# Gate and up slabs of a two-block transformer kernel computed as seven products of halves instead of eight

## The chip, the cores and the metric

The kernel runs on one core of a Trainium2 chip, in one launch. The metric is device time in microseconds, the median of three runs. The profile is one execution taken by the hardware profiler.

## The reference

Two blocks run one after the other on 256 tokens of width 1024, in float32. The first block has two layers, and carries two streams of 256 tokens: the latents (`lat`) and a context (`cx`). Each layer puts both streams through a gated feed-forward, a token mixer with a two-way scan over chunks, and a second feed-forward. The second block has attention, a convolution, a memory attention and a mixture of 32 experts. The change touches the feed-forwards of the first block alone:

```python
D_MODEL = 1024; SEQ = 256; DEPTH = 2; D_FF = 2816
def _swiglu(h, w1, w3, w2):
    return (jax.nn.silu(h @ w1) * (h @ w3)) @ w2

lat = lat + 0.5 * ml[2] * _swiglu(_modulate(lat, norm_ffn1_g[l], ml[0], ml[1]), *ffn1)
cx  = cx  + 0.5 * mc[2] * _swiglu(_modulate(cx,  norm_ffn1_g[l], mc[0], mc[1]), *ffn1)
...
lat = lat + 0.5 * ml[8] * _swiglu(_modulate(lat, norm_ffn2_g[l], ml[6], ml[7]), *ffn2)
```

## The kernel before

The work is cut into **slabs**, one for each 1 MB piece of weights. A gate slab is 256 output columns of `w1` (128 partitions x 8 blocks of the contraction x 256 columns), an up slab the same of `w3`. A feed-forward has 11 pairs of one gate and one up slab, and then 12 down slabs. A **run** is named by (layer, stream, which of the two feed-forwards): stream 0 is the latents, held in `h`, stream 1 the context, held in a part of `ring` that the loads don't use.

The order is one list of stages, made by `first_order` (L196 to L268) and walked by each engine with its own code: TensorE, ScalarE, VectorE, GpSimd and the load queue each take from it what is theirs, strictly in that order, and wait for each other by semaphores. `spread_out` puts a **side chain** between the slabs of a run, one bundle of stages after a slab: in the runs (0,0,0), (0,1,1) and (1,1,0) it is a scan of the other stream's mixer. For each of four heads it holds two `decay` stages (VectorE makes exponents; at the odd one ScalarE takes their exponential, L1552 to L1554), `times` (VectorE L1771, GpSimd L2427), two `score` stages (TensorE L1191 to L1208, VectorE reduces), `value` and `head`. The run (0,0,0) has in its stream (0,1) a `gmlp` stage (TensorE L1172, VectorE L1777) ahead of the first decay.

A gate or up slab on TensorE (L1122) is 16 matrix products of 128x128 weights with 256 columns of tokens, into one of four PSUM banks. The profile shows every float32 product as two MATMUL rows, so that a slab is 32 rows. Behind a gate slab ScalarE writes `sil`, the silu of the bank (L1486). Behind an up slab VectorE multiplies `sil` with the bank into `hid` (L1771, 128x512). Nothing else of VectorE belongs to a slab, and TensorE waits for either of them only when it comes to the same bank again, four slabs later.

The loads go through a ring of `RING` = 5 places of 1 MB; the load of slab k waits until TensorE has finished slab k-5 (L798). `ada` slabs, which make the modulation vectors, use the same ring but take TensorE about 0.5 us each.

## Time and profile before

| | us |
|---|---|
| median of 3 runs | 3049.12 |
| lowest, highest | 3047.38, 3049.76 |
| span of the profiled execution | 3046.6 |
| TensorE busy | 2881.2 |
| VectorE busy | 916.5 |
| ScalarE busy | 539.0 |
| mean granted clock of TensorE | 0.974 |

The span is the time from the first instruction to the last. The median lies 2.5 us above it, which is what lies around the span. The mixture of experts takes the last 440 us or so; it waits for loads of weights at about 430 GB/s.

### The profile page before, as it was taken

To read this page: it belongs to the slowest core of one execution; us is meant where nothing else is said; L and a number is where in the kernel's file an instruction comes from. 1 tells how busy PE (TensorE), PEld (TensorE's weight loads), DVE (VectorE), ACT (ScalarE), POOL (GpSimd) and SP (SyncE) were. 2 spreads that over 40 slices of the span, in tenths; PEclk is the share of its full clock that TensorE was granted. 3 is DMA by queue.
4 is the path that set the end of the run, shared out by engine and by line. 5 is a ranking of instruction groups with operands and counts; after the bars stand their busy time and mean duration, and the time that the engine had idled before them with its cause. 6 is when DMAs were issued, how large, how long until landed. Compare 5 with 4: busy or idle time off the path is not lost.

```text
span 3046.6 us, 36306 instructions
## 1 busy us (share of the span) xinstructions
PE 2881.2 (95%) x15970; PEld 2403.4 (79%) x15970; DVE 916.5 (30%) x1686; ACT 539.0 (18%) x784; POOL 120.7 (4%) x192
## 2 busy tenths in 40 slices
PE   8999999999999999999999999999999999866766
PEld 6888888888888888888888888878888888533333
DVE  3864034331433215300014433510036412210111
ACT  2101222123211101010033206210012240200000
POOL 0000012100211000000001210000000000000000
PEclk9999999999999999999999999999999999987788
DMA  9775443344333566554444344354433238899998
GB/s 401 282 270 181 152 140 133 128 152 152 138 135 128 207 249 228 178 218 150 154 152 150 133 144 152 138 223 152 151 138 125 97 104 338 350 431 431 429 430 371
DMA packets 74128, 641.25 MB, mean 210 GB/s; under 512 B 8304, under 2 KB 9584, under 8 KB 21232
## 3 DMA queue, kind: packets, MB, share of 16 engines
q1 hardware_dynamic: 71376, 631.55, 54.8%
q10 hardware_dynamic: 2592, 7.33, 0.6%
q8 instruction: 129, 2.11, 0.3%
q14 instruction: 31, 0.25, 0.0%
HBM read 637.80 MB, written 1.05 MB: 210 GB/s over the span
## 4 chain that ended last, share of the span: by engine, by line
PE 86%; DMA 12%; DVE 1%; issue 0%; ACT 0%; SPq 0%; DVEq 0%; ACTq 0%
PE ps L1122 42%; PE ps L1144 18%; DMA work<-in_w_moe 11%; PE ps L1319 7%; PE ps L1132 3%; PE ps L1155 3%; PE ps L1349 2%; PE ps L953 2%; PE ps L1208 1%; PE ps L975 1%; DMA ring<-in_w_ada 1%; PE ps L1326 1%; PE ps L1080 0%; PE ps L1294 0%; PE ps L1297 0%; PE ps L1385 0%
## 5 line engine op out<-in xcount | busy, mean ns | idle before, releaser
L1122 PE MATMUL ps<-h,ring 128*128 128x256 f32 x3456 | 755.8, 380 | 7.0 <-ACT h L1526 2.9
L1122 PEld LDWEIGHTS ps<-h,ring 128*128 128x128 f32 x3456 | 654.5, 190 | 102.2 <-issue 8.7
L1122 PE MATMUL ps<-ring 128*128 128x256 f32 x2560 | 559.0, 379 | 0.0
L1144 PE MATMUL ps<-work,ring 128*128 128x256 f32 x2464 | 537.8, 379 | 0.0
L1122 PEld LDWEIGHTS ps<-ring 128*128 128x128 f32 x2560 | 484.0, 190 | 67.7 <-issue 1.9
L1144 PEld LDWEIGHTS ps<-work,ring 128*128 128x128 f32 x2464 | 466.3, 190 | 64.5 <-issue 2.1
L1771 DVE TENSOR_TENSOR work<-work,ps 128x512 f32<-128x512 f32 (+1 forms) x153 | 88.0, 575 | 713.9 <-PE ps L1122 637.6
L1319 PE MATMUL ps<-h,ring 128*128 128x256 f32 x928 | 205.0, 379 | 0.5 <-DVE h L1777 0.5
L1319 PEld LDWEIGHTS ps<-h,ring 128*128 128x128 f32 x928 | 174.8, 190 | 27.5 <-issue 4.2
L1777 DVE SCALAR_TENSOR_TENSOR work<-work,ring 128x1024 f32<-128x1024 f32 x140 | 173.5, 1281 | 1.7
L1486 ACT ACTIVATE work<-ps 128x512 f32<-128x512 f32 x77 | 46.0, 597 | 707.4 <-PE ps L1122 707.3
L1771 DVE TENSOR_TENSOR work<-work 128x128 f32<-128x128 f32 (+5 forms) x449 | 154.8, 401 | 47.5 <-ACT eb L1554 24.9
L2427 POOL TENSOR_TENSOR work<-work 128x128 f32<-128x128 f32 x168 | 100.0, 632 | 1690.3 <-ACT work L1552 1690.3
L953 PE MATMUL ps<-ring,work 128*32 128x256 f32 x1024 | 73.9, 452 | 34.2 <-DMA ring<-in_w_moe 33.9
L953 PE MATMUL ps<-work 128*32 128x256 f32 x992 | 71.6, 444 | 36.5 <-DMA work<-in_w_moe 35.8
L953 PEld LDWEIGHTS ps<-ring,work 128*32 128x32 f32 x1024 | 40.7, 129 | 66.6 <-issue 54.0
L953 PEld LDWEIGHTS ps<-work 128*32 128x32 f32 x992 | 40.1, 127 | 66.2 <-issue 53.2
L1777 DVE SCALAR_TENSOR_TENSOR x<-ps,mod,x 128x256 f32<-128x256 f32 x48 | 21.0, 480 | 234.2 <-PE ps L1144 166.0
L975 PE MATMUL ps<-work 128*32 128x512 f32 x288 | 49.7, 855 | 29.9 <-DMA work<-in_w_moe 29.5
L1730 ACT ACTIVATE work<-ps 32x256 f32<-32x256 f32 x64 | 24.0, 374 | 299.3 <-PE ps L953 298.9
L2368 DVE COPY work<-ps 128x128 f32<-128x128 f32 x32 | 9.3, 292 | 214.1 <-PE ps L962 214.1
L1349 PE MATMUL ps<-work,ring 128*128 128x256 f32 x320 | 70.2, 380 | 1.6 <-DVE work L1771 1.6
(287 smaller groups left out, 2176.8 us busy)
## 6 DMA issues: line engine op xcount, KB each, us to landing
ring<-in_w SPq DMA_DIRECT2D x182, 1024.0 KB, 4.8
work<-in_w_moe SPq DMA_DIRECT2D x22, 4096.0 KB, 33.6
ring<-in_w_moe SPq DMA_DIRECT2D x22, 4096.0 KB, 33.2
ring<-in_w_in SPq DMA_DIRECT2D x80, 1024.0 KB, 4.8
ring<-in_w SPq DMA_DIRECT2D x56, 896.0 KB, 4.7
work<-in_w_ada SPq DMA_DIRECT2D x40, 1024.0 KB, 6.8
ring<-in_w_ada SPq DMA_DIRECT2D x32, 1024.0 KB, 4.9
ring<-in_w_out SPq DMA_DIRECT2D x16, 1024.0 KB, 4.9
```

The lines of the kernel that those rows point to most:

```text
L953: last = nc.tensor.matmul(ps[i * CAP:i * CAP + CAP, g % 2, 0:256], hg[:, q % 2, k, e * CAP:e * CAP + CAP], w[i][:, k * 256:k * 256 + 256], ...
L975: last = nc.tensor.matmul(ps[e * CAP:e * CAP + CAP, 2 + half, :], hv[:, q % 2, e, k, :], w[e][:, k * 512:k * 512 + 512], start=(k == 0), s ...
L1122: last = nc.tensor.matmul(ps[:, b, c * L:c * L + L], w[:, k * L + c * P:k * L + c * P + P], hs[cols][:, k, :], start=(k == 0), stop=(k == ...
L1132: last = nc.tensor.matmul(ps[:, b, t * L:t * L + L], hs[stage[2]][:, k, t * P:t * P + P], w[:, k * L:k * L + L], start=(k == 0), stop=(k = ...
L1144: last = nc.tensor.matmul(ps[:, b, c * L:c * L + L], w[:, k * L + c * P:k * L + c * P + P], hid[:, k0 + k, :], start=(k0 + k == 0 and c == 0),
L1155: last = nc.tensor.matmul(ps[:, b, c * L:c * L + L], w[:, k * L + c * P:k * L + c * P + P], hs[s][:, k, :], start=(k == 0), stop=(k == KD ...
L1319: last = nc.tensor.matmul(ps[:, b, c * L:c * L + L], w[:, k * L + c * P:k * L + c * P + P], hs[0][:, k, :], start=(k == 0), stop=(k == KD ...
L1349: last = nc.tensor.matmul(ps[:, b, c * L:c * L + L], w[:, k * L + c * P:k * L + c * P + P], src[:, k, :], start=(k == 0), stop=(k == kn - 1))
L1486: nc.scalar.activation(sil[:, nth % 2, :], ps[:, b, :], ACT.Silu).then_inc(ev_a, 1)
L1771: return nc.vector.tensor_tensor(o, i0, i1, op)
L1777: return nc.vector.scalar_tensor_tensor(o, i0, s, i1, op0, op1)
L2427: nc.gpsimd.tensor_tensor(keys, keys, k_in, ALU.mult)
```

## The change

64 of the 154 gate and up slabs are computed in another way, a form of Strassen's product with seven products of halves in place of eight (`HALVED`): pairs 1 to 10 of the run (1,0,0), pairs 2 to 10 of (1,0,1), pairs 3, 5, 7, 9 of (0,0,0) and of (1,1,0), pairs 2, 4, 6, 8, 10 of (0,1,1). The slab's weights are four quarters, b11 to b22 (4 blocks of the contraction by 128 columns), the tokens four quarters, a11 to a22 (4 blocks by 128 tokens). `ON_POOL` is empty, so that all sums are VectorE's.

- `halves`, once for each run: VectorE makes s1 to s4, sums and differences of the quarters of the tokens, four operations of 128x512.
- `combine`, once for each slab: VectorE makes t3, b12-b11, t2 and t4 of the quarters of the weights, four operations of 128x512. It stands ahead of the slab before its own.
- TensorE: 28 products of 128x128 weights with 128 columns, into two banks, bx and by. The first two groups need only the weights and tokens, the third waits for `halves`, the next three for `combine`, and the last for `one_out`.
- ScalarE: a copy of one quarter of bx (128x128), which is `one_out`; behind a gate slab then a silu of the sums in SBUF.
- VectorE: three sums of 128, 128 and 256 elements and one of 384 for each slab; behind an up slab the product into `hid`.
- The ring has 4 places for loads in place of 5; the fifth holds the sums of the weights.

```diff
-RING = 5
+RING = 4
+HALVED = {(0, 0, 0): range(3, 11, 2), (0, 1, 1): range(2, 11, 2), (1, 1, 0): range(3, 11, 2), (1, 0, 0): range(1, 11), (1, 0, 1): range(2, 11)}
...
+def with_halves(plan):
...
+        ready = max(n for n in range(slabs[mine[0]]) if plan[n] == ("norm", l, s, 2 * j))
+        busy = [n for n in range(slabs[mine[0]]) if plan[n][0] == "gmlp"]
+        at = max([slabs[mine[0] - 2], ready + 1] + ([busy[-1] + 1] if l == 0 else []))
+        before[at].append(("halves", *run))
+        for i in mine:
+            before[max(slabs[i - 1], at)].append(("combine", *plan[slabs[i]]))
...
+                        product(bx, 3, b11, a11)
+                        product(bx, 0, b21, a12)
+                        pe.wait_ge(halves_done, at.halves_at[stage[1:4]] + 1)
+                        product(bx, 2, b22, s4).then_inc(x_mm, 1)
+                        engine, made = at.combined[stage]
+                        pe.wait_ge(combined_p if engine == "p" else combined_d, made)
+                        product(by, 2, b12, s1)
+                        product(by, 1, t3, s3)
+                        product(by, 0, t2, s2).then_inc(y_mm, 1)
+                        pe.wait_ge(one_out, nth + 1)
+                        product(bx, 1, t4, a22).then_inc(fb_slab, 1)
...
+                    elif is_halved(stage):
+                        nth, which = at.gate_at[stage[1:]][1], int(kind == "up")
+                        act.wait_ge(x_mm, at.halved[n] + 1)
+                        if not which:
+                            act.wait_ge(ev_d, at.up_at[nth - 1])
+                        nc.scalar.activation(part_sums[:, which, 1, :], ps[:, at.group[n] % 4, 3 * P:4 * P], ACT.Copy
+                                             ).then_inc(one_out, 1)
+                        if not which:
+                            act.wait_ge(ev_d, at.sums_at[n])
+                            nc.scalar.activation(sil[:, 0, :], sil[:, 0, :], ACT.Silu).then_inc(ev_a, 1)
...
+                    elif kind == "combine" and not on_pool(stage[1:]):
...
+                        tt(t3, b12, b22, sub).then_inc(dve_own, 1)
+                        third = S.next(dve_own)
+                        tt(b12, b12, b11, sub)
+                        dve.wait_ge(dve_own, third)
+                        own(tt(t2, b11, t3, sub))
+                        tt(t4, b21, t2, sub).then_inc(combined_d, 1)
+                    elif is_halved(stage):
...
+                        dve.wait_ge(one_out, at.halved[n] + 1)
+                        dve.wait_ge(y_mm, at.halved[n] + 1)
+                        own(tt(both[:, 0, :], both[:, 1, :], ps[:, by, 0:P], add))
+                        own(tt(both[:, 2, :], both[:, 0, :], ps[:, by, P:2 * P], add))
+                        tt(both[:, 3:5, :], pair, ps[:, by, 2 * P:3 * P].unsqueeze(1).to_broadcast([P, 2, P]), add).then_inc(ev_d, 1)
+                        dve.wait_ge(fb_slab, at.slab[n] + 1)
+                        dve.wait_ge(ev_d, at.sums_at[n] - 1)
+                        tt(total[:, 0:3 * P], total[:, 0:3 * P], ps[:, bx, 0:3 * P], add).then_inc(ev_d, 1)
```

**TensorE, run (0,0,0), from the `gmlp` stage on.** Before, slab 3 of this run (gate of pair 3) follows as 16 products of 256 columns:

```order
L1172 MATMUL ps<-wsbs,work 128x128 [waits gm_v,const_in]
L1172 MATMUL ps<-wsbs,work 128x128 x7
L1122 MATMUL ps<-h,ring 128x256 [waits w_full2,ev_a]
L1122 MATMUL ps<-h,ring 128x256 x15
L1122 MATMUL ps<-h,ring 128x256 [waits w_full3,ev_a]
L1122 MATMUL ps<-h,ring 128x256 x15
```

The same place in the changed kernel:

```order
L1286 MATMUL ps<-wsbs,work 128x128 [waits gm_v,const_in]
L1286 MATMUL ps<-wsbs,work 128x128 x7
L1214 MATMUL ps<-h,ring 128x128 [waits w_full2,ev_a]
L1214 MATMUL ps<-h,ring 128x128 x7
L1214 MATMUL ps<-work,ring 128x128 [waits halves_done]
L1214 MATMUL ps<-work,ring 128x128 x3
L1214 MATMUL ps<-work,ring 128x128 [waits combined_d]
L1214 MATMUL ps<-work,ring 128x128 x11
L1214 MATMUL ps<-h,work 128x128 [waits one_out]
L1214 MATMUL ps<-h,work 128x128 x3
```

The slab now stops at three places inside itself for VectorE and ScalarE.

**VectorE, the same run, from the `gmlp` stage to the first decay.** Before, the decay (L1786 is its first line) follows at once:

```order
L1771 TENSOR_TENSOR work<-work,ps 128x512
L1777 SCALAR_TENSOR_TENSOR pmt<-ps,vec,wsbs 128x256 x4
L1771 TENSOR_TENSOR ring<-pmt,work 128x1024
L1786 SCALAR_TENSOR_TENSOR work<-ring,work 128x256
L1771 TENSOR_TENSOR be<-work 128x2
```

In the changed kernel:

```order
L1895 TENSOR_TENSOR ring<-pmt,work 128x1024
L1895 TENSOR_TENSOR work<-h 128x512 x2
L1895 TENSOR_TENSOR work<-work,h 128x512
L1895 TENSOR_TENSOR work<-h,work 128x512
L1895 TENSOR_TENSOR ring<-ring 128x4x128 x3
L1895 TENSOR_TENSOR work<-ring 128x512
L1910 SCALAR_TENSOR_TENSOR work<-ring,work 128x256
```

`halves` (three rows) and the `combine` of gate 3 (two rows) have moved in ahead of it.

**VectorE, the same run, between the first decay and the second.** Before:

```order
L2009 COPY work<-work 128x2x64
L1771 TENSOR_TENSOR work<-work 128x2x64 x2
L1771 TENSOR_TENSOR work<-be,work 128x2x64
L1786 SCALAR_TENSOR_TENSOR work<-ring,work 128x256
L1771 TENSOR_TENSOR be<-work 128x2
```

In the changed kernel:

```order
L1895 TENSOR_TENSOR work<-be,work 128x2x64
L1895 TENSOR_TENSOR ring<-ring 128x4x128 x3
L1895 TENSOR_TENSOR work<-ring 128x512
L1895 TENSOR_TENSOR work<-work,ps 128x128 x2
L1895 TENSOR_TENSOR work<-work,ps 128x256
L1895 TENSOR_TENSOR work<-work,ps 128x384
L1910 SCALAR_TENSOR_TENSOR work<-ring,work 128x256
```

The `combine` of up 3 (two rows) and the four sums of gate 3 (three rows), which wait for TensorE, now stand between the two decays.

**ScalarE, the same run, around the second decay.** Before, the exponentials stand between the silus of gates 3 and 4 (L1486), and TensorE needs neither at once:

```order
L1486 ACTIVATE work<-ps 128x512 [waits ev_d,fb_slab] x2
L1552 ACT_TABLE_LOAD
L1552 ACTIVATE work<-work 128x2304 [waits dec_in]
L1553 ACTIVATE work<-work 128x2304
L1554 ACTIVATE eb<-be 128x4
L1486 ACT_TABLE_LOAD [waits ev_d]
L1486 ACTIVATE work<-ps 128x512 [waits fb_slab]
```

In the changed kernel:

```order
L1600 ACTIVATE work<-ps 128x128 [waits ev_d,x_mm]
L1604 ACTIVATE work<-work 128x512 [waits ev_d]
L1676 ACT_TABLE_LOAD
L1676 ACTIVATE work<-work 128x2304 [waits dec_in]
L1677 ACTIVATE work<-work 128x2304
L1678 ACTIVATE eb<-be 128x4
L1600 ACTIVATE work<-ps 128x128 [waits x_mm]
L1610 ACT_TABLE_LOAD [waits ev_d]
```

The copy of up 3 (the second L1600), for which TensorE waits inside the slab, stands behind the three exponentials.

## Rows read from the trace of the kernel before

**Rows 1.** The page: busy us (share), chain by engine, VectorE's wait for TensorE.
```profile
span 3046.6 us, 36306 instructions
PE 2881.2 (95%) x15970; PEld 2403.4 (79%) x15970; DVE 916.5 (30%) x1686; ACT 539.0 (18%) x784; POOL 120.7 (4%) x192
PE 86%; DMA 12%; DVE 1%; issue 0%; ACT 0%; SPq 0%; DVEq 0%; ACTq 0%
L1771 DVE TENSOR_TENSOR work<-work,ps 128x512 f32<-128x512 f32 (+1 forms) x153 | 88.0, 575 | 713.9 <-PE ps L1122 637.6
```

**Rows 2.** Timeline, TensorE: start, length, line, out<-in, shape, count; four stretches.
```profile
416.56 1.95 PE L1172 MATMUL ps<-wsbs,work 128*128 128x128 f32 x16
418.35 27.79 PE L1122 MATMUL ps<-h,ring 128*128 128x256 f32 x128
...
2239.07 3.73 PE L1027 MATMUL ps<-ones 128*128 128x128 f32 x32
2670.52 3.84 PE L861 MATMUL ps<-st,pmt 128*128 128x128 f32 x32
```

**Rows 3.** Groups by line and form, VectorE: count, then busy us, mean ns of one.
```profile
L1771 DVE TENSOR_TENSOR h<-x,rs 128x256 f32<-128x256 f32 x48 | 16.6, 420 | 2.4 <-ACT rs L1519 2.4
L1771 DVE TENSOR_TENSOR ring<-ring 128x512 f32<-128x512 f32 x15 | 10.4, 694 | 9.7 <-ACT ring L1510 9.1
L2078 DVE COPY st<-ps 128x128 f32<-128x128 f32 x8 | 2.3, 290 | 9.5 <-issue 5.8 <-PE ps L1276 3.6
```

**Rows 4.** Timeline: eight sums in a row on VectorE, and a ScalarE copy.
```profile
465.79 0.38 ACT L1603 ACTIVATE ring<-ps 128x256 f32<-128x256 f32 x1 [9.88 <-PE ps L1229]
...
1043.85 2.77 DVE L1771 TENSOR_TENSOR h<-x,rs 128x256 f32<-128x256 f32 x8 [0.48 <-ACT rs L1519]
```

**Rows 5.** Timeline, all engines, run (0,0,0) from the end of up 2.
```profile
416.76 0.69 DVE L1771 TENSOR_TENSOR work<-work,ps 128x512 f32<-128x512 f32 x1 [24.25 <-PE ps L1122]
...
420.32 1.23 DVE L1771 TENSOR_TENSOR ring<-pmt,work 128x1024 f32<-128x1024 f32 x1
421.58 0.69 DVE L1786 TENSOR_TENSOR_SCAN work<-ring,work 128x256 f32<-128x256 f32 x1
...
426.13 0.69 DVE L1786 TENSOR_TENSOR_SCAN work<-ring,work 128x256 f32<-128x256 f32 x1
...
430.68 2.12 ACT L1552 ACTIVATE work<-work 128x2304 f32<-128x2304 f32 x1 [3.33 <-DVE work L1771]
...
434.93 1.28 ACT L1486 ACT_TABLE_LOAD   x1
...
445.98 0.60 PE L1191 MATMUL ps<-ident,work 128*128 128x128 f32 x4
```

**Rows 6.** Timeline, all engines, run (1,1,0) from gate 2 on.
```profile
1611.40 28.87 PE L1122 MATMUL ps<-ring 128*128 128x256 f32 x133
...
1630.00 0.69 DVE L1771 TENSOR_TENSOR work<-work,ps 128x512 f32<-128x512 f32 x1
```

**Rows 7.** Timeline, TensorE, with the idle time before in brackets and its releaser.
```profile
1045.80 4.51 PE L1122 MATMUL ps<-h,ring 128*128 128x256 f32 x12 [1.95 <-DMA ring<-in_w]
1907.94 7.17 PE L1122 MATMUL ps<-h,ring 128*128 128x256 f32 x32 [2.16 <-DVE rs L1774]
2620.81 3.66 PE L953 MATMUL ps<-ring,work 128*32 128x256 f32 x64
2764.01 5.06 PE L953 MATMUL ps<-ring,work 128*32 128x256 f32 x64 [3.23 <-DMA ring<-in_w_moe]
2880.62 6.47 PE L953 MATMUL ps<-ring,work 128*32 128x256 f32 x64 [3.52 <-DMA ring<-in_w_moe]
```

**Rows 8.** Windows: stretch, its us, busy us by engine, granted clock, DMA share, GB/s.
```profile
2580.00:2600.00 20.00, 19.13 (x121) 17.39 (x120) 3.80 (x13) 5.90 (x10) 0.00 (x0) 1.00 0.54 217
2902.70:2904.70 2.00, 2.00 (x28) 0.98 (x23) 0.00 (x0) 0.00 (x0) 0.00 (x0) 0.50 0.95 410
```

**Rows 9.** The page, loads: KB each, median us from issue to landing.
```profile
ring<-in_w SPq DMA_DIRECT2D x182, 1024.0 KB, 4.8
```

130 lines of the change are left out of this document (126 added, 4 removed).

## The prediction, written before the changed kernel had run

> **What bounds the kernel now.** I read the page first: TensorE is busy for 95% of the span and holds 86% of the chain that ended last, loads hold 12%, and VectorE and ScalarE are busy for 30% and 18% [rows 1]. VectorE's 637.6 us of idle time ended by TensorE say the same from the other side: it is VectorE that waits [rows 1]. The timeline of TensorE comes next. Through the feed-forwards it has no gap: four slabs, 128 matrix rows, take 27.79 us [rows 2]. So whatever a slab saves there is saved in the span, and whatever TensorE waits for there is added. The mixture of experts at the end waits for loads of weights, but just ahead of it, in 2580 to 2600, the DMA engines stand at 0.54 of their time [rows 8]: they are out of places to load into, so this last stage begins when the work ahead of it ends, and simply shifts.
>
> **What a slab saves.** The last row of a run of matmuls shows its own latency, so I take the step from row to row. 128 rows of 256 columns take 27.79 us; less the 0.38 of one, over 127 steps, that is 0.2158 us, and a slab of 32 rows is **6.91 us** [rows 2]. The same for 128 columns with a new set of weights in each product: the sixteen rows of L1172 start at 416.56 and the next line starts at 418.35, 0.112 us a row [rows 2]; the 32 rows of L1027 give (3.73-0.28)/31 = 0.1113, and those of L861 (3.84-0.28)/31 = 0.115 [rows 2]. Seven products of halves are 28 products, 56 rows: 6.23 us at 0.1113, 6.44 at 0.115. I take 0.1113, since L1172, which has the same form and a wait in front, is nearest to it. A slab saves 6.91-6.23 = 0.68 us (0.47 at the other end), and 64 slabs **43.2 us** (30 at the other end). It is 10% and not 12.5% because two steps at 128 columns are longer than one at 256.
>
> The row of L1172 shows a new load of weights every 0.112 us beside the matmuls, hidden. The Trainium skill, "TensorE: Matmul & The Clock Gate", section "Back-to-back issue gap", speaks against the change: at 128 columns, pairs of a weight load and a matmul sustain about 81 ns where the matmul alone would take 56, that is 1.45 times. That rule's result is the last rival below.
>
> **What the added work costs where nothing else is in the way.** VectorE: one 128x512 sum in SBUF takes 0.69 us [rows 3]. Eight sums of 256 in a row take 2.77 us, a step of 0.34 where one alone is 0.42 [rows 3, 4], so independent ones overlap by 0.08 and I count 0.61 where nothing is waited for. A `combine` is then 0.61+0.61+0.72+0.61 = 2.55 us, ready for TensorE at 2.65; `halves` are 0.72+0.61+0.72+0.61 = 2.66, ready at 2.77. The three small sums are 0.32+0.32+0.46 (a 128-wide operation on PSUM is 0.29, a 256-wide one 0.42 [rows 3]), the last about 0.5, the product into `hid` 0.65: 1.6 us for a gate slab, 2.3 for an up slab. With two combines that is 9.0 us for a pair of slabs in which TensorE works 12.5 us. In the runs (1,0,0) and (1,0,1), which have nothing else on VectorE, a combine ends about 4.0 us after the end of the slab two before its own, and TensorE needs it 6.23+2.67 = 8.9 us after the same point. So VectorE is hidden by 5 us there, and 38 slabs give their whole 25.7 us. Where the slabs begin, behind `ada` slabs, I find one wait of 0.4 us.
>
> **The waits beside the scans.** TensorE's last product of a slab waits for ScalarE's copy, 5.34 us after the slab's start, and ScalarE takes its stages in order. Where an odd decay stands ahead of the copy, its exponentials do too, and they wait for VectorE's decay. A decay is 4.55 us on VectorE (421.58 to 426.13), the exponentials 4.25 us on ScalarE (430.68 to 434.93) [rows 5], the copy about 0.3 (0.38 for 256 columns [rows 4]): from a decay's start to TensorE's going on are 9.15 us.
>
> (0,0,0), pair 3, with times of the profile: VectorE ends `gmlp` at 421.55 [rows 5]. `halves` are ready at 424.35, so TensorE, which starts gate 3 at 418.35 and has 1.78 us of products that don't need them, waits 4.2 us. The combine comes at 426.9: 1.6 more. Gate 3 ends at 430.5. VectorE: first decay to 431.3, combine of up 3 to 433.9 (TensorE waits 0.9), sums of gate 3 to 435.5, second decay to 440.05; exponentials and copy to 444.6. TensorE has come to its last product of up 3 at 436.7: **8.0 us**. Before, this hurt nobody: VectorE's second decay ran from 426.13, and TensorE needed its result at 445.98 [rows 5]. Pair 9 has the same form without `halves`: let gate 9 start at 0. The even decay ends at 4.6, the combine of up 9 at 7.2, the sums at 8.8, the odd decay at 13.35, the copy at 17.9; TensorE is there at 6.23+5.34 = 11.6: 6.35 us. Pairs 5 and 7 meet `score` stages or an odd decay that is over in time, and wait for nothing. Sum 21.1 us.
>
> (0,1,1): pair 2 waits 1.1 us twice for combines behind the decays; pair 4 is pair 9 again, 6.35; gate 8 has the odd decay ahead of it (VectorE begins it 0.85 us after up 7, TensorE gets its copy at 10.0 and is there at 5.35): 4.65. Sum 13.2.
>
> (1,1,0): VectorE is late already, since the gating chain keeps it to 1630.0, where up 2 had ended at 1611.40+13.82 = 1625.2 [rows 6]. Behind it now come `halves` (ready at 1632.7, where TensorE stands at 1627.0: 5.7 us), the combine of gate 3 (1.65), and then, in the order of pair 3 above, decay, combine of up 3 (1.5), sums, second decay, copy at 1653.7, where TensorE stands at 1645.75: 8.0. Gate 7 is gate 8 of the other run: 4.5. Sum 21.35.
>
> All **55.6 us** of waits are TensorE's own and nothing in these stretches gives them back; the savings of the same 26 slabs are 17.6 us. What comes late next, GpSimd's products behind the exponentials and then `score`, has two or more slabs to go.
>
> **The clock.** After an idle time of 3.23 us a group of 64 rows takes 5.06 us where it takes 3.66 otherwise, after 3.52 it takes 6.47 [rows 7]; in such a stretch the granted clock stands at 0.50, that is 1.2 GHz [rows 8]. After 1.95 and 2.16 us of idleness nothing of the kind is seen (7.17 us for 32 rows, where 31 steps and a latency make 7.07) [rows 7]. So each wait of 4.5 us or more costs 1.4 to 2.8 us again. There are eight over 4 us; behind the two for `halves` the slow products end before VectorE has come to the next point, which leaves six: **12.6 us** at 2.1 each, 8 to 17.
>
> **The ring.** Loads run one slab less ahead. With 6.2 to 6.9 us a slab and 4.8 us from issue to landing [rows 9] nothing waits. Where five `ada` slabs of 0.5 us come together it does: at 1045.80 TensorE waits 1.95 us for a load already [rows 7]. There are three such places and the start; a load of 1 MB takes 2.4 us at 430 GB/s, and each place may lose up to one such. I take **4 us**, bounds 0 and 9.
>
> **The sum.** -43.2+55.6+0.4+12.6+4 = +29.4 us. On the profiled span, 3046.6 becomes 3076.0; the median of the runs lies 2.5 us above the span: **3078 us**.
>
> **The rivals.** (a) The clock doesn't fall, since a part of the products is done between the waits, and the ring costs nothing: -43.2+56 = +12.8, 3062 us. For it: no row shows a gap of 4 us in the middle of dense work; against it: the granted clock fell behind each gap of over 3 us that I saw. (b) **Faster**: the waits are half of what I walked. The one mechanism that could do it is ScalarE's copy coming ahead of the odd decay's exponentials. The places are the up slabs of pair 3 (in both runs), 9 and 4 and the gates 7 and 8. Without these 37.85 us of waits the clock falls behind the two waits for `halves` alone: -43.2+17.75+0.4+4+4 = -17, 3032 us. It decides from the point where waits and clock together are under 39 us. The order of ScalarE's instructions speaks against it. (c) The halves run at 0.115 us a row: 13 us more, 3092 us; three stops inside each slab speak for it, rows across a change of line that show no gap speak against it. (d) The slab is not shortened at all but the waits stay: 64 x 0.68 us are missing, 3122 us; that is the case in which the change doesn't do what it says. (e) Weight loads set the pace: 56 rows at 1.45 x 0.108 = 0.157 us are 8.8 us a slab, 1.9 longer than before, and with the waits 3049+120+73 = 3242 us. This is the Trainium skill's rule from above, and the sixteen rows at 0.112 say no.
>
> **How the numbers follow.** The forecast has a chance of 0.56 with its own bounds, 3066 to 3090. (a) has 0.12, (b) 0.16, (c) 0.12, (d) 0.03, (e) 0.01. The range of 80% leaves out (d), (e) and most of (b), and takes in (c) with the upper bounds of clock and ring: 3045 to 3100. A measurement of this kernel can tell 0.2%, 6 us, from no change. Faster: 0.12, three quarters of (b). Within 0.2%: 0.07, the rest of (b) and the lowest part of (a). Slower: 0.81.
>
> **What would show it.** Right: L1214 in groups of 56 rows, 6.2 us apart without waits; TensorE's idle time at L1214 of 50 to 60 us, released by ScalarE's copy (some 38 us, six times over 4 us) and by VectorE (some 18 us); a granted clock under 1.00 behind them; in (1,0,0) and (1,0,1) no idle time. Wrong: a step above 0.113 us in dense halves, waits for the copy under 3 us, or idle time in the layer-1 latent runs, which would mean that I have VectorE too fast.

## The result and the profile after

The changed kernel takes **3084.84 us** (median of 4 runs, 3083.68 to 3086.87), the kernel before 3049.42: 1.0119 times as long, 95% interval 1.0105 to 1.0134. That is 35.4 us more; 29 were forecast.

The page of the changed kernel (span; busy us and share by engine; chain by engine), the lines that answer to [rows 1]:

```profile
span 3081.3 us, 40170 instructions
PE 2858.2 (93%) x17506; PEld 2432.4 (79%) x17506; DVE 1192.9 (39%) x2218; ACT 557.1 (18%) x848; POOL 126.7 (4%) x192
PE 80%; DMA 13%; DVE 5%; ACT 1%; issue 1%; SPq 0%; DVEq 0%; ACTq 0%
```

TensorE does less work and the span is longer. VectorE, at 39% of its time, now holds 5% of the chain that ended last, and ScalarE 1%. The list of TensorE's waits (line, what released it: us in total, times, longest) says where:

```profile
PE ps L1214 <- ACT work L1600: 34.7, 6, 7.5
PE ps L1161 <- DMA ring<-in_w_ada: 18.2, 11, 9.2
PE ps L1214 <- DVE work L1895: 14.7, 8, 5.6
```

L1214 is the products of halves. Six times TensorE waited for ScalarE's copy, 34.7 us, and eight times for sums or combines of VectorE, 14.7 us. L1161 is the `ada` slabs: 18.2 us of waits for their loads.

The timeline of TensorE in a latent feed-forward of layer 1 (start, length, line, shape, count) is what [rows 2] were for plain slabs:

```profile
1378.00 1.95 PE L1214 MATMUL ps<-h,ring 128*128 128x128 f32 x16
1379.79 3.74 PE L1214 MATMUL ps<-work,ring 128*128 128x128 f32 x32
1383.36 1.06 PE L1214 MATMUL ps<-h,work 128*128 128x128 f32 x8
1384.25 1.95 PE L1214 MATMUL ps<-h,ring 128*128 128x128 f32 x16
```

Three rows are one slab: 56 matmuls, no idle time, the next slab 6.25 us later. Over fifteen slabs in a row, 1378.00 to 1471.80, it is 6.253 us, 0.1117 us a row.

The timeline of TensorE beside the first scan, run (0,0,0), with the idle time ahead of a row in brackets:

```profile
423.69 1.61 PE L1214 MATMUL ps<-work,ring 128*128 128x128 f32 x8 [4.08 <-DVE work L1895]
426.23 5.23 PE L1214 MATMUL ps<-work,ring 128*128 128x128 f32 x24 [0.92 <-DVE work L1895]
431.30 1.06 PE L1214 MATMUL ps<-h,work 128*128 128x128 f32 x8
432.19 1.95 PE L1214 MATMUL ps<-h,ring 128*128 128x128 f32 x16
433.98 3.74 PE L1214 MATMUL ps<-work,ring 128*128 128x128 f32 x32
443.78 2.08 PE L1214 MATMUL ps<-h,work 128*128 128x128 f32 x8 [6.07 <-ACT work L1600]
445.65 15.21 PE L1236 MATMUL ps<-h,ring 128*128 128x256 f32 x64
```

The first wait is for `halves`, the second for the combine of gate 3, the third for ScalarE's copy behind the exponentials. The eight products of 443.78 take 2.08 us where the same eight take 1.06 at 431.30: the clock has fallen. It is the granted clock in the windows (us, busy us by engine, granted clock, DMA share, GB/s) that says so:

```profile
444.00:446.00 2.00, 2.00 (x9) 1.99 (x10) 0.86 (x4) 0.00 (x0) 2.00 (x6) 0.50 0.00 0
446.00:448.00 2.00, 2.00 (x6) 1.56 (x5) 1.90 (x3) 0.60 (x1) 2.00 (x4) 0.50 0.52 123
448.00:450.00 2.00, 2.00 (x10) 1.74 (x10) 2.00 (x2) 0.68 (x1) 2.00 (x2) 0.97 0.95 401
```

**Where the time went**, by the start of the same stage in the two timelines (after less before; a difference of differences is what the stretch added):

| stretch | added, us | of it: halved slabs' saving | waits at L1214 | rest |
|---|---|---|---|---|
| up to the first halved slab | -0.7 | | | -0.7 |
| run (0,0,0) | +20.0 | 8 x 0.655 = -5.2 | 17.3 | 7.9 |
| run (0,1,1) | +11.0 | 10 x 0.655 = -6.6 | 13.5 | 4.1 |
| `ada` slabs 1037 to 1061 | +3.3 | | | 3.3 |
| `ada` slabs 1287 to 1302 | +5.2 | | | 5.2 |
| run (1,0,0) | -12.4 | 20 x 0.655 = -13.1 | 0.4 | 0.3 |
| run (1,1,0) | +19.6 | 8 x 0.655 = -5.2 | 18.3 | 6.5 |
| `ada` slabs at 1996 | +0.5 | | | 0.5 |
| run (1,0,1) | -11.8 | 18 x 0.655 = -11.8 | 0 | 0 |

Behind the last of these every stage starts 34.6 us later than before, to the end. Beside the scans 26 halved slabs save 17.0 us and lose 49.0 in waits and 18.5 in the column "rest". Most of that rest is slow products: in these three runs TensorE works 31.7 us while the granted clock stands at 0.50, and at full clock the same work takes half of it, so that 15.9 us are the clock's: 11.1 behind the six waits for copies, 4.8 behind the two for `halves`. Each stop also lets the last product ahead of it show its latency, 0.17 us (32 products take 3.74 us, 32 steps 3.57); for thirteen stops that is an estimate of 2.2 us. Of the 9.0 us at the `ada` slabs 4.7 are longer waits and 3.8 slow products behind them (TensorE works 11.0 us at 0.50 there, and 3.4 in the kernel before).

### The profile page after: what moved, and what is told of

The parts are those of the page before. It is cut to its first block, busy times and chain, and to the rows that moved or that the text cites. A ratio compares the mean times of both kernels' runs of the same rounds, so it can differ in the third digit from the quotient of the medians.

```text
span 3081.3 us, 40170 instructions
## 1 busy us (share of the span) xinstructions
PE 2858.2 (93%) x17506; PEld 2432.4 (79%) x17506; DVE 1192.9 (39%) x2218; ACT 557.1 (18%) x848; POOL 126.7 (4%) x192
## 4 chain that ended last, share of the span: by engine, by line
PE 80%; DMA 13%; DVE 5%; ACT 1%; issue 1%; SPq 0%; DVEq 0%; ACTq 0%
PE ps L1236 27%; PE ps L1258 17%; DMA ring<-in_w_moe 11%; PE ps L1214 11%; PE ps L1433 7%; PE ps L1246 3%; PE ps L1269 3%; PE ps L1463 2%; DVE work L1895 2%; PE ps L1034 2%; PE ps L1322 1%; DMA ring<-in_w_ada 1%; PE ps L1440 1%; PE ps L1161 1%; DVE ring L1895 1%
## 5 line engine op out<-in xcount | busy, mean ns | idle before, releaser
L1258 PE MATMUL ps<-work,ring 128*128 128x256 f32 x2464 | 537.8, 379 | 0.0
L1258 PEld LDWEIGHTS ps<-work,ring 128*128 128x128 f32 x2464 | 466.1, 190 | 64.4 <-issue 2.1
L1236 PE MATMUL ps<-h,ring 128*128 128x256 f32 x1984 | 440.4, 383 | 5.0 <-DVE rs L1898 2.2
L1236 PE MATMUL ps<-ring 128*128 128x256 f32 x1984 | 436.0, 381 | 0.1
L1236 PEld LDWEIGHTS ps<-h,ring 128*128 128x128 f32 x1984 | 379.2, 192 | 62.3 <-issue 6.7
L1236 PEld LDWEIGHTS ps<-ring 128*128 128x128 f32 x1984 | 376.1, 191 | 53.4 <-issue 1.9
L1895 DVE TENSOR_TENSOR work<-work,ps 128x128 f32<-128x128 f32 (+4 forms) x377 | 164.9, 437 | 503.2 <-PE ps L1236 292.7
L1214 PE MATMUL ps<-work,ring 128*128 128x128 f32 x2048 | 245.4, 278 | 14.7 <-DVE work L1895 14.7
L1214 PEld LDWEIGHTS ps<-work,ring 128*128 128x128 f32 x2048 | 238.6, 195 | 16.4 <-DVE work L1895 16.4
L1433 PE MATMUL ps<-h,ring 128*128 128x256 f32 x928 | 204.9, 379 | 0.5 <-DVE h L1901 0.5
L1433 PEld LDWEIGHTS ps<-h,ring 128*128 128x128 f32 x928 | 174.8, 190 | 27.5 <-issue 4.2
L1895 DVE TENSOR_TENSOR work<-work 128x128 f32<-128x128 f32 (+5 forms) x481 | 177.3, 420 | 36.0 <-ACT work L1669 13.9
L1895 DVE TENSOR_TENSOR ring<-ring 128x512 f32<-128x512 f32 x207 | 136.0, 707 | 15.0 <-ACT ring L1634 9.1
L1034 PE MATMUL ps<-work 128*32 128x256 f32 x992 | 72.4, 448 | 34.7 <-DMA work<-in_w_moe 34.1
```

The costliest lines, as they stand in the source:

```text
L1034: last = nc.tensor.matmul(ps[i * CAP:i * CAP + CAP, g % 2, 0:256], hg[:, q % 2, k, e * CAP:e * CAP + CAP], w[i][:, k * 256:k * 256 + 256], ...
L1214: last = nc.tensor.matmul(ps[:, b, place * P:place * P + P], weight[:, k, :], act[:, k, :], start=(k == 0), stop=(k == 3), skip_group_chec ...
L1236: last = nc.tensor.matmul(ps[:, b, c * L:c * L + L], w[:, k * L + c * P:k * L + c * P + P], hs[cols][:, k, :], start=(k == 0), stop=(k == ...
L1258: last = nc.tensor.matmul(ps[:, b, c * L:c * L + L], w[:, k * L + c * P:k * L + c * P + P], hid[:, k0 + k, :], start=(k0 + k == 0 and c == 0),
L1433: last = nc.tensor.matmul(ps[:, b, c * L:c * L + L], w[:, k * L + c * P:k * L + c * P + P], hs[0][:, k, :], start=(k == 0), stop=(k == KD ...
L1895: return nc.vector.tensor_tensor(o, i0, i1, op)
```

## The experiments

Each was timed in turn with the kernel before on the same chip; two chips were used, and the kernel before had medians of 3049.1 to 3049.3 us in all of them.

### ring4: one ring place less, nothing else

The kernel before with four places in its ring; the place's memory stays taken, as in the change.

```diff
-RING = 5
+RING = 4
-        ring = sb("ring", [P, AHEAD + RING, SLAB])
+        ring = sb("ring", [P, AHEAD + RING + 1, SLAB])
```

> The kernel before with one edit: loads go through 4 places in place of 5, no slab is halved. My theory: the three places where TensorE waited longer for loads behind the ada slabs (offsets of 3.3, 5.2 and 0.5 us between the two traces) come from the ring alone, less 0.7 us won at the start: 3049.4+8.3 = 3057.7 us. Rival: the ring costs nothing, and what the changed kernel lost there comes from the changed work around it: 3049 us.

Measured: 3060.33 us, ratio 1.0032 (1.0020 to 1.0044). **11 us**, 2.6 us above the theory and far from the rival. TensorE's waits at the `ada` slabs are 5 in the kernel before and 8 here (first fence: before, second: ring4), and its timeline at one burst is the third:

```profile
PE ps L1080 <- DMA ring<-in_w_ada: 11.8, 5, 9.5
```

```profile
PE ps L1080 <- DMA ring<-in_w_ada: 14.0, 8, 9.5
```

```profile
1044.64 1.07 PE L1080 MATMUL ps<-ring 128*32 128x256 f32 x16 [0.39 <-DMA ring<-in_w_ada]
1047.09 1.07 PE L1080 MATMUL ps<-ring 128*32 128x256 f32 x16 [1.38 <-DMA ring<-in_w_ada]
1049.62 12.73 PE L1122 MATMUL ps<-h,ring 128*128 128x256 f32 x44 [1.46 <-issue]
```

In place of the one wait of 1.95 us at the end of such a burst [rows 7], TensorE stops at each of the last loads. By the starts of the stages the three bursts cost 3.0, 4.9 and 0.5 us, where the theory took 3.3, 5.2 and 0.5. The profile is 12.0 us longer than that of the kernel before; of the rest, 1.7 us each are slow products near 93 us and behind a wait at 1918 for VectorE. `latents5` (below), which has all five places, has both as well, so it isn't shown that they belong to the place's price: 8 to 9 us are shown for it, and 11 are measured in all.

### latents5 and latents: only the layer-1 latents, with five places and with four

The two latent runs alone are halved (38 slabs). In `latents5` the mixed sums lie in a part of the work area that is free outside the scans, and the ring keeps its five places; `latents` has the changed kernel's four.

```diff
-HALVED = {(0, 0, 0): range(3, 11, 2), (0, 1, 1): range(2, 11, 2), (1, 1, 0): range(3, 11, 2), (1, 0, 0): range(1, 11), (1, 0, 1): range(2, 11)}
+HALVED = {(1, 0, 0): range(1, 11), (1, 0, 1): range(2, 11)}
```
and in `latents5` also
```diff
-RING = 4
+RING = 5
-        ring = sb("ring", [P, AHEAD + RING + 1, SLAB])
+        ring = sb("ring", [P, AHEAD + RING, SLAB])
-        mixed = [shaped(ring[:, AHEAD + RING, i * 8 * P:i * 8 * P + 8 * P], 4, 2, P) for i in range(2)]
+        mixed = [shaped(work[:, lf_at + i * 8 * P:lf_at + i * 8 * P + 8 * P], 4, 2, P) for i in range(2)]
```

> The change in the two layer-1 latent feed-forwards alone (38 slabs), none beside a scan, and with 5 places for loads: the sums of the weights stand in a part of the work area that is free there. My theory: 38 slabs save 0.655 us each, one wait of 0.4 us, no clock loss: 3049.4-24.5 = 3025 us. Rival: the halves are dearer than their rows show or VectorE holds TensorE up as soon as every pair is halved: 3035 us or more.

> Only the slabs of the two layer-1 latent feed-forwards are halved (38 of them), as in the run latents5, but with the changed kernel's four ring places in place of five. Theory (a ring of four costs its 9 to 11 us at the adaptation slabs whatever else is changed): 3025.3 + 9 to 11 = 3034 to 3037, with 9 to 12 us of waits for the DMA of w_ada at TensorE. Rival (the ring costs nothing by itself beside halved slabs, since a halved slab leaves the DMA less time per slab and so both rings run dry alike): 3025 to 3028.

Measured: `latents5` 3025.32 us, ratio 0.992 (0.9904 to 0.9935): 24 us **faster** than the kernel before, the whole of 38 x 0.655 = 24.9. `latents` 3037.93, 0.996 (0.9947 to 0.9974): by the medians 12.6 us of it are lost again to the ring, by the spans of the two profiles 7.7 (the runs of `latents` lie 7 us apart). `latents5` is what its theory said; `latents` is 1 us above its theory and 10 from its rival. So the loss of the place is there beside halved slabs as it is without them.

### latents5_vector and latents5_vector2: how much room VectorE has there

`latents5` with the last sum of every combine written four times more, and twice more; the repetitions write the same values.

```diff
                         own(tt(t2, b11, t3, sub))
+                        for _ in range(4):
+                            own(tt(t4, b21, t2, sub))
                         tt(t4, b21, t2, sub).then_inc(combined_d, 1)
```

> The run latents5 with the last sum of each combine (128x512) written four times more, each waiting for the one before: about 4 x 0.7 = 2.8 us more on VectorE in each of the 38 halved slabs. Theory (outside the scans VectorE has slack: a slab takes 6.25 us of TensorE and its sums and combine about 4 us of VectorE, and the combine runs a slab ahead): the time stays 3025 +- 3. Rival (the halved slabs run at VectorE's pace, or the combine is late as soon as it takes longer): 38 x 1 to 2.8 us more, 3060 to 3130, with waits at L1214 for DVE.

Measured: 3071.57 us, ratio 1.0073 (1.0059 to 1.0087). **My theory fell**: 2.9 us more for each slab cost 46 us, 1.22 for each of the 38. TensorE's list of waits and VectorE's timeline of this run:

```profile
PE ps L1214 <- DVE work L1895: 32.7, 31, 3.3
```

```profile
1407.81 0.69 DVE L1895 TENSOR_TENSOR ring<-ring 128x512 f32<-128x512 f32 x1
1408.41 4.32 DVE L1895 TENSOR_TENSOR work<-ring,work 128x512 f32<-128x512 f32 x6
1412.64 1.71 DVE L1895 TENSOR_TENSOR work<-work,ps 128x128 f32<-128x128 f32 x4
1414.81 0.69 DVE L1895 TENSOR_TENSOR work<-work 128x512 f32<-128x512 f32 x1 [0.46 <-DVE work L1895]
```

VectorE has no idle time left but that 0.46 us inside its own chain. The same engine in `latents5`:

```profile
1400.82 1.72 DVE L1895 TENSOR_TENSOR work<-work,ps 128x128 f32<-128x128 f32 x4 [2.00 <-PE ps L1214]
1404.46 1.41 DVE L1895 TENSOR_TENSOR work<-ring,work 128x512 f32<-128x512 f32 x2
1407.08 1.72 DVE L1895 TENSOR_TENSOR work<-work,ps 128x128 f32<-128x128 f32 x4 [1.20 <-PE ps L1214]
```

It is idle 1.20 and 2.00 us in turn, 3.2 of the 12.5 us of a pair of slabs. Four sums of 0.72 are 5.8 us a pair; less the 3.2, 2.6 are too many, 1.3 a slab. The theory had taken the time by which one combine is early (5 us) for the time that VectorE has free (1.6 us a slab). From this the second run:

> The run latents5 with the last sum of each combine written twice more, in place of four times: 2 x 0.72 = 1.44 us more on VectorE in each of the 38 halved slabs. In latents5 VectorE is idle for 1.2 and 2.0 us of two slabs in turn (period 6.25 us), 1.6 us in the mean. Theory (VectorE's queue is the bound only beyond that slack: 4 x 0.72 - 1.6 = 1.3 us for each of 38 slabs is 49 us, measured 46): 1.44 us fit, the time stays 3025 to 3029. Rival (each microsecond on the way from one slab's sums to the next combine counts in part, whatever slack there is): half of 46 us, 3048.

Measured: 3028.07 us, ratio 0.9931 (0.9917 to 0.9944), within the theory and 20 us from the rival. The room is a matter of VectorE's sum of work, and it ends 1.6 us above what the change gives it.

### copy_first: ScalarE's copy ahead of the exponentials

The changed kernel, in which ScalarE holds back an odd head's exponentials where the next slab is a halved one, until it has made that slab's copy.

```diff
+                        while held:
+                            decay(held.pop())
...
-                        act.wait_ge(dec_in, 4 * PASS[l, s] + hd // 2 + 1)
-                        nc.scalar.activation(ex[:, 0, :, :], ex[:, 0, :, :], ACT.Exp).then_inc(dec_out, 1)
...
+                        if is_halved(next(later for later in plan[n:] if is_slab(later))):
+                            held.append(stage)
+                        else:
+                            decay(stage)
```

> The changed kernel, but ScalarE takes its copy of a halved slab ahead of an odd decay's three exponentials wherever that slab follows the decay; the order of VectorE and TensorE is as it was. My theory: the six waits for the copy (34.7 us idle) go, and the clock's loss behind them; what stays are the waits for the sums of tokens and weights, and the clock's loss behind two of them: 3084.8-48 = 3037 us. Rival: VectorE's longer chain is what holds TensorE, and the copy only comes last: the waits move to VectorE's sums, 3065 us or more.

Measured: 3044.92 us, ratio 0.9986 (0.9977 to 0.9995): 40 us faster than the changed kernel, 8 short of the theory. Five of the six copy waits are gone and the last is 0.2 us; VectorE's stay:

```profile
PE ps L1214 <- DVE work L1906: 14.8, 8, 5.6
PE ps L1305 <- issue: 2.4, 1, 2.4
PE ps L1236 <- DMA ring<-in_w: 2.2, 1, 2.2
PE ps L1214 <- ACT work L1610: 0.2, 1, 0.2
```

The transposes of `score` (L1305) now wait 2.4 us, at 1660.44, where neither the kernel before nor the changed one has a wait. ScalarE's new order isn't what does it: `late` (below), which has the old order, waits 2.10 us at the same place. They wait for GpSimd's products behind the exponentials. The kernel before, then `late`:

```profile
1641.90 8.29 POOL L2427 TENSOR_TENSOR work<-work 128x128 f32<-128x128 f32 x14 [694.30 <-ACT work L1552]
```

```profile
1649.81 11.45 POOL L2612 TENSOR_TENSOR work<-work 128x128 f32<-128x128 f32 x14 [684.31 <-ACT work L1676]
1663.03 0.41 PE L1305 MATMUL ps<-ident,work 128*128 128x128 f32 x2 [2.10 <-issue]
```

Wherever none of VectorE's sums of weights or tokens falls into them, the fourteen products take 8.3 us (8.75 once in `warm`), in all traces; with four to six of these sums beside them they take 9.8 to 10.8 (10.51 at this place here), with eight 11.45. The sums are longer too. Two combines of the changed kernel, without GpSimd at work and with it (808.08 to 818.34):

```profile
805.77 1.88 DVE L1895 TENSOR_TENSOR ring<-ring 128x512 f32<-128x512 f32 x3
813.26 2.67 DVE L1895 TENSOR_TENSOR ring<-ring 128x512 f32<-128x512 f32 x3
```

So 2.2 of the 2.4 us are GpSimd's longer time (10.51 less 8.29), and TensorE comes there sooner, since its waits are gone. This is read from the traces; no run was made to part the two engines. By stage, it is 40.4 us ahead of the changed kernel at 1719.66, and gives 3.6 back at two waits outside the scans; the next run has the same two. The profile is of the slowest of its ten runs (3049.51 us).

### warm: the clock behind the copy waits

In the same six waits TensorE multiplies ones by ones, 15 to 26 times, into a place of PSUM that nothing reads.

```diff
-                        product(by, 0, t2, s2).then_inc(y_mm, 1)
+                        last = product(by, 0, t2, s2)
+                        for _ in range(WARM.get(stage[:5], 0)):
+                            last = nc.tensor.matmul(ps[:, by, 3 * P:4 * P], ones[:], ones[:], start=True, stop=True,
+                                                    skip_group_check=True)
+                        last.then_inc(y_mm, 1)
```

> The changed kernel, with 15 to 26 products of ones by ones (128x128, f32) put into the row of TensorE in six of the halved slabs beside the scans, right before it waits for ScalarE's copy (in the waits of 4.1, 6.1, 6.2, 6.2, 7.5 and 4.3 us of the changed kernel's trace); nothing reads what they write. Theory (12 to 19 us of the loss are the clock that falls behind these waits): TensorE works through most of each wait, the clock stays up, the idle time before L1214 falls from 49 to some 20 us with the products of ones in its place, and the time falls by the clock's share of the copy waits, about 10 to 15 us: 3071 to 3075. Rival (the clock term is a mistake and the waits are all of the loss): 3085, with the granted clock as it was. Second rival (the products of ones outlast the waits and cost their own time): above 3088.

Measured: 3077.39 us, ratio 1.0095 (1.0080 to 1.0110): 7.4 us less than the changed kernel, a little short of the range. The timeline at the place that was shown above:

```profile
435.66 3.74 PE L1215 MATMUL ps<-work,ring 128*128 128x128 f32 x32
439.24 5.08 PE L1229 MATMUL ps<-ones 128*128 128x128 f32 x44
445.54 1.16 PE L1215 MATMUL ps<-h,work 128*128 128x128 f32 x8 [1.22 <-ACT work L1605]
446.53 13.98 PE L1241 MATMUL ps<-h,ring 128*128 128x256 f32 x64
```

L1229 is the 22 products of ones, two rows of the profile each. The wait for the copy is as long as it was (6.3 us from their start to going on), but the products behind it take 1.16 and 13.98 us, where they took 2.08 and 15.21. That is 2.15 us for this one wait. Behind the three scans the kernel is 9.0 us ahead of the changed one (at 1751.05; in this 1.7 us lost near 91 us and 1.8 won at the `ada` slabs cancel). Then it falls back by 3.6, at two waits outside the scans that both kernels have. The first of them in `warm`, and in the changed kernel:

```profile
1944.90 1.65 PE L1241 MATMUL ps<-h,ring 128*128 128x256 f32 x3 [2.16 <-DVE rs L1903]
```

```profile
1953.87 7.17 PE L1236 MATMUL ps<-h,ring 128*128 128x256 f32 x32 [2.16 <-DVE rs L1898]
```

The same idle time; three matmuls take 1.65 us in the one, 32 take 7.17 in the other, the length of full clock. The windows behind them (granted clock in the third column from the end), `warm`, then the changed kernel:

```profile
1945.00:1947.00 2.00, 2.00 (x5) 1.63 (x6) 1.63 (x1) 0.34 (x1) 0.00 (x0) 0.50 0.04 16
```

```profile
1954.00:1956.00 2.00, 2.00 (x10) 1.77 (x11) 1.60 (x1) 0.37 (x1) 0.00 (x0) 1.00 0.00 0
```

Whether it falls there doesn't go by the edit. All fourteen profiles of this study have this wait of 2.16 us; in seven (before, changed, `latents`, both `latents5_vector`, `late`, `lent5_all`) the 32 matmuls behind it take 7.17 us and in the other seven 8.78 to 8.86. So I take the 9.0 us as the clock's share of the copy waits, and the 3.6 as chance. The granted clock agrees: behind the six copy waits TensorE worked 22.2 us at 0.50 in the changed kernel, 11.1 us of loss, and none in `warm`, where it fell once more behind a wait for VectorE instead (814.50, 1.7 us).

### late and copy_first_late: the first pairs left plain

The first halved pair of each scan's run is computed as before, so that the halved pairs begin two pairs later, where VectorE has worked off what it was behind: 58 slabs. `late` is this alone, `copy_first_late` this on top of `copy_first`.

```diff
-HALVED = {(0, 0, 0): range(3, 11, 2), (0, 1, 1): range(2, 11, 2), (1, 1, 0): range(3, 11, 2), (1, 0, 0): range(1, 11), (1, 0, 1): range(2, 11)}
+HALVED = {(0, 0, 0): range(5, 11, 2), (0, 1, 1): range(4, 11, 2), (1, 1, 0): range(5, 11, 2), (1, 0, 0): range(1, 11), (1, 0, 1): range(2, 11)}
```

> As copy_first, and the first halved pair of each run beside a scan is computed as before (58 slabs halved in place of 64). My theory: with the first pairs go all waits for the sums of the tokens and nearly all for those of the weights (some 19.5 us with the clock), for 3.9 us less saved: 3037-15.6 = 3021 us. Rival: the next pair meets the same waits: 3037 us or more.

Measured: 3027.22 us, ratio 0.9922 (0.9907 to 0.9937). VectorE's waits are down to 0.4 us, and the time is 17.7 us less than `copy_first` although 6 slabs are plain again: by the medians VectorE's waits cost about 21.6 us, 14.4 of them idle. Of the rest 6.4 us are slow products: beside the scans TensorE works 12.8 us at a granted clock of 0.50 in `copy_first`, and not at all here. The gain is 2 us more than the 15.6 expected; the time is 6 us above the theory, because the `copy_first` from which it was reckoned lay 8 above its own.

> The changed kernel with the first one or two halved pairs of each scan's run left plain (pairs 5, 7, 9 in the runs (0,0,0) and (1,1,0), pairs 4, 6, 8, 10 in (0,1,1)): 58 halved slabs in place of 64. ScalarE's order is the changed kernel's. Theory (a wait costs its own length and about 2 us of clock behind it, and the terms add): the waits for VectorE's sums go, and with them 17.7 us (what copy_first_late gained on copy_first, the 6 slabs that are plain again taken off); of the copy waits the two of 6.1 and 7.5 us go, with 2 us of clock behind each, four stay: 3084.8 - 17.7 - 18 = 3049. Rival (the copy is late wherever the first halved pair stands, so that pairs 5 wait in place of pairs 3): 3084.8 - 17.7 = 3067.

Measured: 3056.17 us (11 runs, 3049.55 to 3059.59), ratio 1.0023 (1.0014 to 1.0032). By the waits the theory is right and the rival, pairs 5 in the place of pairs 3, is wrong: the list has four copy waits, those of pair 9, pair 4, gate 8 and gate 7.

```profile
PE ps L1214 <- ACT work L1600: 21.2, 4, 6.2
```

By the time it is 7 us above the theory. The runs differ by 10 us, and with them the granted clock that each recorded: 0.973 in the lowest, 0.968 in the highest. The profile is of a run of 3051.2 us, 2 above the theory; what the slower runs lose stands in no trace. That the loss behind one and the same wait differs is shown by a wait of 4.3 us in two kernels, `late` and the changed one:

```profile
1703.86 2.08 PE L1214 MATMUL ps<-ring,work 128*128 128x128 f32 x8 [4.27 <-ACT work L1600]
1705.73 3.62 PE L1214 MATMUL ps<-ring 128*128 128x128 f32 x16
```

```profile
1737.33 1.16 PE L1214 MATMUL ps<-ring,work 128*128 128x128 f32 x8 [4.26 <-ACT work L1600]
1738.33 3.58 PE L1214 MATMUL ps<-ring 128*128 128x128 f32 x16
```

The clock falls in both (the sixteen products take 1.95 at full clock), in the one with the wait and in the other a microsecond after it. From going on to the next slab it is 9.81 us in the one and 8.88 in the other.

### lent5: the fifth place back

`copy_first_late` with five ring places. The fifth is lent to the mixed sums only from three slabs ahead of a scan's first halved slab to four behind its last, and carries slabs everywhere else; the latent runs mix in the work area. A load then waits for the slab that last used its place, in place of the one RING before.

```diff
+    narrow = {k: run for run in runs for k in range(run[0] - 3, run[1] + 5)}
+    for k in range(at.slabs):
+        free = [i for i in last if not (k in narrow and i == RING - 1)]
+        place = min(free, key=lambda i: -1 if last[i] is None else last[i])
...
-                    if k >= RING:
-                        sp.wait_ge(fb_slab, k - RING + 1)
+                    if users[k] is not None:
+                        sp.wait_ge(fb_slab, users[k] + 1)
...
-            m = mixed[nth % 2]
+            if stage[1:4] in LATENTS:
+                m = mixed_l[nth % 2]
+            else:
+                m = shaped(ring[:, lent, nth % 2 * 8 * P:nth % 2 * 8 * P + 8 * P], 4, 2, P)
```

> The run copy_first_late with five ring places: the fifth is lent to the mixed sums only in the stretches of the scans' halved slabs and carries slabs everywhere else (the latent runs keep their mixed sums in the work area, as in latents5). 58 halved slabs. Theory (the terms add: 58 slabs x 0.66 us saved, the waits gone, the ring's loss at the adaptation slabs gone too): 3027.2 - 9 to 11 = 3016 to 3018, and the waits for w_ada at TensorE back to what the kernel before has (2 to 4 us). Rival (the loss of the ring falls in the stretches where the place is lent, or the change of places costs new waits for DMA): 3024 to 3030.

Measured: **3017.98 us** (3017.55 to 3018.62), ratio 0.990 (0.9885 to 0.9915). 31 us under the kernel before, 67 under the changed one. That is the upper end of the theory. Against `copy_first_late` it gains 4.1, 4.6 and 2.5 us at the three bursts of `ada` slabs, by the starts of the stages, and loses 1.5 us beside the last scan, where the clock falls behind the wait for `score` and didn't in `copy_first_late`. These of TensorE's waits bear on it (L1339 is that wait, for GpSimd as above; 9.2 us of the first line are the start of the program):

```profile
PE ps L1195 <- DMA ring<-in_w_ada: 12.5, 8, 9.2
PE ps L1339 <- issue: 2.1, 1, 2.1
PE ps L1270 <- DMA ring<-in_w: 1.5, 1, 1.5
```

### lent5_ends and lent5_all: more pairs

```diff
-HALVED = {(0, 0, 0): range(5, 11, 2), (0, 1, 1): range(4, 11, 2), (1, 1, 0): range(5, 11, 2), (1, 0, 0): range(1, 11), (1, 0, 1): range(2, 11)}
+HALVED = {(0, 0, 0): (5, 7, 9, 10), (0, 1, 1): (4, 6, 8, 9, 10), (1, 1, 0): (5, 7, 9, 10), (1, 0, 0): range(1, 11), (1, 0, 1): range(2, 11)}
```
and in `lent5_all`
```diff
+HALVED = {(0, 0, 0): range(5, 11), (0, 1, 1): range(4, 11), (1, 1, 0): range(5, 11), (1, 0, 0): range(1, 11), (1, 0, 1): range(2, 11)}
```

> The run lent5 with the last pairs of the scans' runs halved too (pair 10 in (0,0,0) and (1,1,0), pair 9 in (0,1,1)): 64 halved slabs. Theory (the last pairs stand where the heads' work has thinned out, so VectorE follows): 6 x 0.65 = 3.9 us less than lent5, 3014 +- 1.5. Rival (VectorE is as late there as anywhere beside a scan): 3018 to 3025 with waits for DVE at the halved slabs.

> The run lent5 with every pair from the fifth (from the fourth in (0,1,1)) of the scans' runs halved, not every second: 76 halved slabs in place of 58, so that the 18 more would save 18 x 0.65 = 11.7 us. Beside the scans VectorE is idle for 10 to 13 us of each 40 us in lent5, and a halved slab takes 4.7 us of it against 1.3 us of two plain evacuations: 3.4 us more for each, of which 3 or 4 lie in 40 us. Theory (VectorE has the time on average but not where the heads' work stands in its queue: a slab's sums wait behind a head's products): the gain is eaten by waits at the halved slabs, 3018 to 3040. Rival (the queue evens out): 3006 to 3010.

Measured: `lent5_ends` 3022.23 us, ratio 0.9911 (0.9896 to 0.9926), 4 us slower than `lent5` where I expected 4 less; `lent5_all` 3031.30, 0.9942 (0.9928 to 0.9956). The last pairs are no better a place than the others. In `lent5_ends`:

```profile
536.61 4.57 PE L1248 MATMUL ps<-work,ring 128*128 128x128 f32 x24 [2.30 <-DVE work L1940]
```

A wait of 2.30 us, and the 24 products behind it take 4.57 us where they take 2.94 behind a shorter one: 3.9 us, six slabs' saving, at one place. The combine that it waits for stands beside GpSimd's products again (they take 10.7 us). The 4 us on top are 2.4 of other waits at halved slabs and 1.8 of waits for loads behind the `ada` slabs; the rival was right. `lent5_all` has eleven waits for VectorE of 15.5 us in all and five for the copy of 3.5, against 11.7 us that its 18 slabs more could save; the time lies in the theory's range. "Every second pair" is thus about what VectorE can follow beside a scan.

## Why the prediction was right, and where its terms were off

The sign, the place and the mechanism held, and the forecast was 7 us short. Two of its terms, the clock and the ring, were too small, and the waits were too large by nearly as much as the clock was too small, so that the total is nearer than its parts.

**What a slab saves.** 0.68 us were forecast by a step of 0.1113 us, 0.655 measured by 0.1117: 41.9 us for 64 slabs in place of 43.2. The three stops inside a slab that were to speak for rival (c) cost nothing visible. Rival (e) is out: 0.1117 us with a new set of weights each is 1.035 times half of a 256-column step (0.2158), not 1.45 times. The Trainium skill, "TensorE: Matmul & The Clock Gate", section "Back-to-back issue gap", gives a time, about 81 ns for each pair at 128 columns, and the factor is what the prediction made of it. A row here takes 112 ns, more than that, so the page's time itself isn't tested. Rival (d) is out too: `latents5` brought the whole saving.

**The waits beside the scans.** 55.6 us were forecast, 49 came, and all but one of the walk's waits are in the timeline (forecast, then measured): for `halves` 4.2 and 4.08, 5.7 and 5.63; behind the exponentials 8.0 and 6.07, 6.35 and 6.19, 6.35 and 6.19, 4.65 and 4.50, 8.0 and 7.53, 4.5 and 4.26. The small waits for combines were mostly too high: 1.6 and 0.9 in (0,0,0) where 0.92 and none came, 1.65 and 1.5 in (1,1,0) where 0.45 and 0.42 came. In (0,1,1) 1.1 and 1.1 became 0.87 and 1.89; the second combine there stands beside GpSimd's products and takes 3.5 us, where the prediction counted 2.55 for every combine. The step that made the others, and the two of 8.0, too high is one I had not carried through: behind the wait for `halves` TensorE works at half clock, 5.23 us where it takes 2.7, and in that time VectorE catches up. The wait becomes shorter by what the products become longer.

**The clock**, 12.6 forecast and 15.9 measured, was mis-sized for the same reason. The six copy waits cost 11.1 us, less than forecast; the two waits for `halves` cost 4.8, and the step that had put them at nothing failed ("the slow products end before VectorE has come to the next point"). The rows of 423.69 and 426.23 alone are 2.8 us longer than at full clock. Waits and clock together were forecast at 68.2 us, and all that the scans' runs lost beside the saving came to 67.6: the sum was right and its parts were shifted. `warm` shows that the clock is a loss of its own: the copy waits stayed and 9 us went. One reading was wrong from the start: that after 1.95 us of idleness "nothing of the kind is seen". The row of 1045.80 itself [rows 7] has 12 matrix rows in 4.51 us, where 11 steps and a latency make 2.75, and the granted clock of the kernel before stands at 0.50 from 1048 to 1050.

**The ring**, 4 us forecast with a bound of 9, is 9.0 us by the stages and 11 us in `ring4`, the largest miss of the sum. I had argued "may lose up to one load each" and taken less than half, from one wait of 1.95 us in the kernel before. That wait says that the reserve is used up at the end of a burst; a place less makes the reserve too small at each load of it, and the two bursts cost 3.3 and 5.2 us. Waits are 4.7 us of the 9.0, and 3.8 are slow products behind them: the clock falls at these bursts too, which follows from the row misread above and stood in no term of the sum.

**The 7 us**: the span was forecast at 3076.0 and is 3081.3. Of these 5.3 us the ring is +5.0, the saving +1.3, waits and what stands behind them -0.6, and the start of the program, where nothing was changed, -0.7. The rest is the step from span to median, 3.5 us in place of 2.5.

**The rivals.** (b), ScalarE's copy ahead of the exponentials, is what `copy_first` builds. It would have given 3032 by the prediction, which had the ring at 4 and the clock at 4; it gave 3045. Of the 13 us between them some 12 have a place: the ring cost 5.0 us more than counted, the clock beside the scans 2.4 more (6.4), two waits for `score` 3.1, two falls of the clock outside the scans 3.6, and the saving was 1.3 smaller; the waits for VectorE were 3.2 shorter. The statement "what comes late next has two or more slabs to go" was right for the changed kernel. Without the copy waits it is wrong: TensorE is early, and GpSimd's products, which it took at the length that they had before, are 2 to 3 us longer beside VectorE's sums.

**VectorE in the latent runs**: "hidden by 5 us" was right as a delay and no wait came but 0.4 us. As room it would have been wrong by three times; the prediction's own 9.0 us of each 12.5 (9.3 measured) is the number that counts there.

## What to carry to other kernels

An edit that shortens TensorE's work with sums on another engine pays where that engine's queue holds nothing else, and loses where its result stands behind somebody's long stage; walk the queue of every engine that must hand something back inside the shortened piece. Here 38 of 64 slabs made 25 us and 26 lost 50, so the first question is which slabs, not whether. Price a buffer place by itself before giving it up: it cost 8 to 11 us alone, a third to near half of what the good part brought, and it could be lent for the stretches that need it.

How early a result is and how much time its engine has free are two numbers. The first decides on a wait, the second on the pace. And what an operation takes alone isn't what it takes beside another engine: here VectorE's added sums and GpSimd's products lengthened each other by a fifth to two fifths.

## What the runs showed of the hardware

The clock behind a given wait isn't the same in every execution. After 2.16 us of idleness at the same instruction it fell in seven profiles of fourteen, which cost 1.6 to 1.7 us; after 1.95 us it fell in the kernel before [rows 7], at a loss of 1.7 us; after 4.26 and 4.27 us it fell both times, at a loss of 1.7 and 2.7 us. At 2.16 us the prediction had said "nothing of the kind is seen" [rows 7], which was one of two outcomes. How far the runs of a kernel lie apart may come from this: 10 us in `late` (clock 0.968 to 0.973), 7 in `copy_first`, 1 in `lent5` (0.973 to 0.974). Of each kernel there is one trace, so it isn't shown.

VectorE and GpSimd slow each other in some operations. A group of fourteen products on GpSimd takes 8.3 us with none of VectorE's 128x512 sums of weights or tokens beside it, 9.8 to 10.8 with four to six and 11.45 with eight; three such sums take 1.88 us with GpSimd idle and 2.67 with it at work. VectorE's sums of a slab, which read PSUM, take 1.7 us in either case.

TensorE with a new set of weights in each 128-column step kept 0.1117 us a row over fifteen slabs of 56 rows in a row; the loads of weights have rows of their own beside the products (PEld), and TensorE stood idle for none of them.
